# Key pages of a paged attention cache, copied ahead in DRAM and turned by float32r transposes

## The reference

```
hn   = rmsnorm(x) * (1 + sc1) + sh1          # sc, sh, gt from silu(c) @ w_ada
q, k, v, xl, gl = split(hn @ w_in)           # 8 heads of 128, LRU width 1024
attn = stick_breaking(q, k, v)               # the prompt over itself
       # sample b: its 8 tokens, then back over its 8 cached pages:
       for page in reversed(page_table[b]):  # keys and values, 128 rows x 8 heads x 128
           z = q @ cache_k[page].T * scale + bias
           w = exp(log_sigmoid(z) + sums of log_sigmoid(-z) to the right + carry)
           o += w @ cache_v[page]
lru  = rglru(conv4(xl)) * gelu(gl)
x    = x + gt1 * (concat(attn, lru) @ w_out)
x    = x + gt2 * ((gelu(ug) * uv) @ w_down)  # ug, uv = conv3(hn2 @ w_up)
```

## Time and profile before

| | |
|---|---|
| median of 3 runs | 2901.7 us |
| profiled execution, its span | 2902.6 us |
| PE busy | 2828.4 us (97%) |
| DVE, ACT, Pool busy | 1769.2, 1189.4, 280.8 us |
| key page transposes on PE, L1052 and L1056 | 2 x 256, mean 286 and 273 ns |
| page loads | 128 of 512 KB, landing after some 5 us |

### The profile page before, as it was taken

How to read it: one execution, slowest core, us unless ns; L and a number is a source line. 1 busy time by engine, 2 the same in 40 slices (tenths; PEclk the granted TensorE clock), 3 DMA queues, 4 the chain that set the end, 5 groups by cost and what they waited for, 6 DMA issues and landing times.

```text
span 2902.6 us, 60828 instructions
## 1 busy us (share of the span) xinstructions
PE 2828.4 (97%) x24051; PEld 2695.1 (93%) x24051; DVE 1769.2 (61%) x2752; ACT 1189.4 (41%) x1458; POOL 280.8 (10%) x532
## 2 busy tenths in 40 slices
PE   5999999999999999799999999999999999999999
PEld 3689999878888999699999999999999999999999
DVE  3433433544534433888888888888888755555553
ACT  3244444545444322644444444444444422222222
POOL 0000000112221000011111111111111000000000
PEclk9999999999999999899999999999999999999999
DMA  9985555377667655633333333333333633333323
GB/s 360 318 264 168 159 162 167 109 230 233 217 222 235 197 158 169 201 115 100 112 105 113 99 117 105 109 100 117 111 102 106 210 109 108 106 107 110 106 82 110
DMA packets 608980, 444.51 MB, mean 153 GB/s; under 512 B 14569, under 2 KB 556127, under 8 KB 607469
## 3 DMA queue, kind: packets, MB, share of 16 engines
q1 hardware_dynamic: 585602, 363.97, 41.2%
q0 software_dynamic: 22176, 77.86, 8.2%
q10 hardware_dynamic: 1044, 0.43, 0.1%
HBM read 408.14 MB, written 34.06 MB: 152 GB/s over the span
## 4 chain that ended last, share of the span: by engine, by line
PE 92%; DVE 3%; DMA 2%; ACT 2%; issue 1%; SPq 0%; DVEq 0%; ACTq 0%; POOLq 0%
PE ps L808 45%; PE ps L1265 36%; PE ps L824 2%; PE ps L1101 1%; PE ps L1067 1%; PE ps L1052 1%; PE ps L904 1%; PE ps L1056 1%; PE ps L932 1%; DMA wide_act<-in_w_ada_dram 1%; PE ps L848 1%; PE ps L966 1%; DMA page<-in_cache_k_dram 0%; PE ps L944 0%; DMA raw<-in_w_in_dram 0%
## 5 line engine op out<-in xcount | busy, mean ns | idle before, releaser
L1265 PE MATMUL ps<-ops,w_hi 128*128 128x288 f32 x4608 | 921.0, 296 | 0.5 <-DVE w_lo L2334 0.5
L1265 PEld LDWEIGHTS ps<-ops,w_hi 128*128 128x128 f32 x4608 | 741.7, 189 | 0.9 <-DVE w_lo L2334 0.9
L1265 PE MATMUL ps<-ops,w_lo 128*128 128x288 f32 x2304 | 679.4, 295 | 0.0
L1929 DVE TENSOR_TENSOR w_lo<-raw,w_hi 128x1024 fp32r<-128x1024 f32 x240 | 293.2, 1225 | 575.4 <-ACT w_hi L1377 575.3
L808 PE MATMUL ps<-gs,w_hi 128*128 128x288 f32 x3072 | 607.1, 294 | 0.0
L808 PE MATMUL ps<-act_hi,w_hi 128*128 128x288 f32 x1792 | 544.7, 304 | 8.4 <-DVE w_lo L1929 3.1
L808 PE MATMUL ps<-act_lo,w_hi 128*128 128x288 f32 x1792 | 528.9, 295 | 0.0
L808 PE MATMUL ps<-act_hi,w_lo 128*128 128x288 f32 x1792 | 528.1, 295 | 0.0
L1377 ACT ACTIVATE w_hi<-raw 128x1024 fp32r<-128x1024 f32 x240 | 253.4, 1058 | 657.3 <-PE ps L808 639.8
L808 PEld LDWEIGHTS ps<-gs,w_hi 128*128 128x128 f32 x3072 | 490.3, 188 | 0.0
L808 PE MATMUL ps<-gs,w_lo 128*128 128x288 f32 x1536 | 451.3, 294 | 0.0
(11 more groups left out here) (377 smaller groups left out, 3130.7 us busy)
## 6 DMA issues: line engine op xcount, KB each, us to landing
raw<-in_w_up_dram SPq DMA_DIRECT2D x120, 512.0 KB, 4.3
raw<-in_w_down_dram SPq DMA_DIRECT2D x128, 384.0 KB, 3.2
raw<-in_w_in_dram SPq DMA_DIRECT2D x80, 512.0 KB, 5.8
ada_q<-in_w_ada_dram SPq DMA_DIRECT2D x80, 512.0 KB, 5.4
page<-in_cache_v_dram POOLq DMA_DIRECT2D x64, 512.0 KB, 4.7
page<-in_cache_k_dram POOLq DMA_DIRECT2D x52, 512.0 KB, 4.7
ax<-in_w_up_dram SPq DMA_DIRECT2D x48, 512.0 KB, 4.9
wide_act<-in_w_ada_dram SPq DMA_DIRECT2D x22, 1024.0 KB, 12.2
```

The lines of the kernel that those rows point to most:

```text
L1265: mm = pe.matmul(ps[:, bank, 0:HALF], w[slot][:, kk, :], moving(i, kk, low), start=i not in ADDED and kk == 0 and w is w_hi and not low, s ...
L1929: dve.tensor_tensor(w_lo[s][:], raw[s][:], w_hi[s][:].bitcast(F32), ALU.subtract).then_inc(lo_done, 1)
```

## The change

While the q,k,v stage runs, Pool copies all 64 key pages from the cache to an internal DRAM tensor `key_save`, in the order in which they will be used, eight for each head; `COPY_AFTER` gives the number of finished blocks of its head that each of the eight waits for. The stores of a head come after its seventh copy. The key pages are later loaded from `key_save` (so at an address that needs no page number) into `keys_r`, a float32r tensor at the same place as the four homes, and turned with a float32r identity into a float32r view of the same banks. `ident_r` is made by DVE at the beginning of the LRU stage, and PE waits for it once. SP and Pool wait for all copies before they load a first key page. Value pages are loaded as before.

```diff
+COPY_AFTER = (0, 0, 1, 2, 2, 3, 4, 4)
...
 SECOND_LIFE = {
+    "sq2_used": ("filled", 2), "ident_rounded": ("consts", 2),
...
+    key_save = nc.dram_tensor("key_save", (NB * PAGES, P, NH * P), F32, kind="Internal").ap()
...
         temps.close()
+        keys_r = rounded("keys_r", [P, 4, NH, P])
         page = [tmp(f"page{i}", [P, NH, P]) for i in range(4)]
...
+        ident_r = tmp("ident_r", [P, P], F32R)
...
-            sp.wait_ge(sem("pt_loaded"), 16)
+            sp.wait_ge(sem("keys_copied"), 16 * NB * PAGES)
             for k in range(4, 16):
-                b, at = page_of(k)
-                number = sp.value_load(pt[0:1, 8 * b + at:8 * b + at + 1], min_val=0, max_val=npool - 1)
                 sp.wait_ge(sem("left_turned"), k - 3)
                 sp.wait_ge(sem("right_turned"), k - 3)
-                sp.dma_start(page[k % 4][:].rearrange("p h d -> p (h d)"),
-                             ck[bass.ds(number, 1)].rearrange("n p c -> p (n c)")) \
+                sp.dma_start(keys_r[:, k % 4].bitcast(F32).rearrange("p h d -> p (h d)"), key_save[k]) \
                   .then_inc(sem(f"early_page{k % 4}"), 16)
...
-                    mm = pe.transpose(ps[:, b0, j * P:(j + 1) * P], page[n % 4][:, j, :], ident[:])
+                    mm = pe.transpose(ps[:, b0, j * P:(j + 1) * P].bitcast(F32R), keys_r[:, n % 4, j, :], ident_r[:])
...
-                    mm = pe.transpose(ps[:, b0 + 1, j * P:(j + 1) * P], page[n % 4][:, 4 + j, :], ident[:])
+                    mm = pe.transpose(ps[:, b0 + 1, j * P:(j + 1) * P].bitcast(F32R), keys_r[:, n % 4, 4 + j, :], ident_r[:])
...
+            pe.wait_ge(sem("ident_rounded"), again("ident_rounded", 1))
             for p in range(16):
                 point(0, p)
...
             take_mod(5, M_QKV + 35, 3, 7 + NH)
+            dve.tensor_copy(ident_r[:], ident[:]).then_inc(sem("ident_rounded"), 1)
             softplus(NH)
...
+            def page_number(n):
+                b, at = page_of(n)
+                return pool.value_load(pt[0:1, 8 * b + at:8 * b + at + 1], min_val=0, max_val=npool - 1)
+
+            def copy_keys(n):
+                pool.dma_start(key_save[n], ck[bass.ds(page_number(n), 1)].rearrange("n p c -> p (n c)")).then_inc(sem("keys_copied"), 16)
...
+                if k is None:
+                    ins = pool.dma_start(page[n % 4][:].rearrange("p h d -> p (h d)"),
+                                         cvv[bass.ds(number, 1)].rearrange("n p c -> p (n c)"))
+                else:
+                    ins = pool.dma_start(keys_r[:, n % 4].bitcast(F32).rearrange("p h d -> p (h d)"), key_save[k])
+                ins.then_inc(sem(f"page_loaded{n % 4}"), 16)
...
-            with pool.Fori(1, NH) as i:
-                store(i)
             pool.wait_ge(sem("pt_loaded"), 16)
+            for i in range(NH):
+                for c in range(8):
+                    wait(pool, blk_used, 6 * i + COPY_AFTER[c])
+                    copy_keys(8 * i + c)
+                    if i and c == 6:
+                        store(i)
+            pool.wait_ge(sem("keys_copied"), 16 * NB * PAGES)
             pool.wait_ge(sem("ada_used"), 10 * NH)
             for p in range(4):
                 load(0, p)
```

More of the change, by code:

```diff
@@ L308, in tmp, with rounded @@
         return temps.enter_context(nc.sbuf_tensor(name, shape, dt))
+    def rounded(name, shape):
+        alone = ExitStack()
+        t = alone.enter_context(nc.sbuf_tensor(name, shape, F32R))
+        alone.close()
+        return t
     names = {}
@@ L1761, in _ @@
             turns(act, 4, out, 4)
-            act.wait_ge(sem("sq2_used"), 1)
+            act.wait_ge(sem("sq2_used"), again("sq2_used", 1))
             act.activation(flat2(rs2[:]), ps[:, 5:7, 0:HALF], ACT.Ln, bias=eps[:], scale=-1.0 / D).then_inc(sem("rs2_ready"), 1)
@@ L2670, in _ @@
             cvv = cache_v[0].rearrange("n p h d -> n p (h d)")
+            def page_number(n):
[3 more added lines that the diff above has]
+                pool.dma_start(key_save[n], ck[bass.ds(page_number(n), 1)].rearrange("n p c -> p (n c)")).then_inc(sem("keys_copied"), 16)
             def load(i, p):
                 k, v, n = key_page(i, p), value_page(i, p), unit(i, p)
-                b, at = page_of(v if k is None else k)
-                number = pool.value_load(pt[0:1, 8 * b + at:8 * b + at + 1], min_val=0, max_val=npool - 1)
+                if k is None:
+                    number = page_number(v)
                 if n >= 4:
@@ L2683, in load @@
                         pool.wait_ge(sem("right_turned"), uses(*q) + 1)
-                pool.dma_start(page[n % 4][:].rearrange("p h d -> p (h d)"),
-                               (cvv if k is None else ck)[bass.ds(number, 1)].rearrange("n p c -> p (n c)")) \
-                    .then_inc(sem(f"page_loaded{n % 4}"), 16)
+                if k is None:
+                    ins = pool.dma_start(page[n % 4][:].rearrange("p h d -> p (h d)"),
[3 more added lines that the diff above has]
+                ins.then_inc(sem(f"page_loaded{n % 4}"), 16)
             def gates(i):
```

## The result

The changed kernel takes 2917.05 us (median of 5 runs, 2913.61 to 2917.53); the kernel before, timed with it, 2905.45 (5 runs). The ratio is 1.0037, its 95% interval 1.0026 to 1.0049: 11 us slower, beyond the 0.2% that counts as no change. The profiled execution spans 2914.7 us, 12.1 more than before.

The account below looks back on a forecast made before the run. TensorE (PE) was taken as the bound, 92% of the chain, with DMA engines full at the q,k,v stage's beginning. 2902.6 - 10.7 + 7.4 = 2899.3, less 0.9 to the runs' median: 2898.4 us, range 2884 to 2914.

Parts of the forecast that it names:

- the price of the burst: Beginning of q,k,v stage: 13 copies in a row delay weight block 12, PE stalls 5.9 us plus 1.5 of clock: 7.4.
- The share of the weights: Beside the copies at 165.0 to 184.8 us, the hardware queue was to move 172 packets a us instead of 626.
- The packets of a copy: Copies into key_save were priced like Pool's page loads, 4 KB a row, at 84 packets a us.
- The length: Burst from 165.0 us: 13 copies, 1664 packets at 84 a us, lasting 19.8 us to 184.8.
- Chunk 8: Weight chunk queued ahead of block 12, needed at 182.9 us: claimed just in time, no stall of its own.
- The clock: After PE's idle gap before head 1's sums, lower granted clock was to cost 1.5 us.
- Rival 4: Copies cost twice a page load's packet time; burst 39.6 us, stall with clock 27.2 us, total 2918.2; chance 0.13.
- The transposes: LRU stage: 512 float32r key transposes start 85 ns apart instead of 109; 10.7 us gained with the first stretch.
- The 48 later pages: Key pages turned between LRU products, counted as PE's time: 48 x 8 x 24 ns = 9.2 us gained.
- the first stretch: First 16 key pages of the LRU stage: faster turning limited by page loads and bandwidth, 1.5 us gained.
- The copies of later heads, ident, the stores and copy 63: q,k,v stage and LRU beginning: later copies hidden, ident copy in idle DVE time, stores and last copy early enough: nothing.

Follow-up runs that it names:

- Experiment 1: Changed kernel with each key_save row 64 bytes longer, so copies go in packets of 4 KB or less: 2914.89 us, 1.0036 of the kernel before.
- experiment 2: Changed kernel with all 64 copies in heads 2 to 7, none in heads 0 and 1: 2898.13 us, 0.9978 of the kernel before.
- experiment 3: Changed kernel with copied pages turned by float32 transposes and the old identity: 2922.4 us, 1.0059 of the kernel before.
- experiment 5: Changed kernel with all copies in heads 2 to 7 and float32 transposes of the copied pages: 2905.22 us, 1.0001 of the kernel before.
- experiment 8: Changed kernel with no copies in heads 0 and 1, 15 in a row at head 3, 9 or 10 in other heads: 2908.51 us, 1.0009 of the kernel before.

## Why the prediction was wrong

- **The term that failed is the price of the burst**, in the copies' part: "13 copies are 1664 packets, at 84 a us 19.8 us", with the hardware queue at 172 rows a us beside them, and hence 7.4 us. It measured 19.1. Place and kind of wait were as forecast: the sums of head 1 waiting for DVE behind a raw block. Three sizes were off, in the same direction.
  1. *The share of the weights.* 172 rows a us came from 600 to 606 us, taken as one state. It is a mixture. From 603 to 604 us of the same trace, where the page loads hold most of the engines, the packets are

```profile
q0 software_dynamic: 90, 0.36, 86.6%
...
q1 hardware_dynamic: 96, 0.05, 16.0%
```

     about one for one, some 90 rows a us. In the other five microseconds the page loads' share is 68 to 78% and 136 to 217 rows go, so for parts of them, by inference, SP's queue alone had work. Experiment 1 shows nearly the same, 80, beside copies in 4 KB packets.
  2. *The packets of a copy.* It was taken to go like a page load, 4 KB a row. Between two contiguous pieces of DRAM it goes in 16 packets of 32 KB, so the weights had 18 rows a us, not 80. This alone was worth little (experiment 1: the sums gained 0.5 us).
  3. *The length.* 14 copies went in a row and a 15th at 185.11, where 13 were counted: blocks 8 and 9 of head 1 were finished meanwhile. And the 84 packets a us include the small ones that end each engine's share, 16 a copy, which "1664 packets" left out. 15 x 144 packets at 80 to 84 a us are 26 to 27 us, which is what both bursts lasted (to 191 or 192 us), not 19.8.

  An estimate in the prediction's own form, with the 4000 packets at 626 a us behind the burst, tells what these are worth. With the measured length alone (26.5 us at 172 rows a us) block 12 lands at 188.3 us, with the measured share alone (19.8 us at 18) at 190.6, with both at 197.1. It landed at 196.4 (issued at 166.51, 29.9 us to landing), where 185.8 was forecast. So length and share made the loss together, and neither alone.
- **A step was left out.** "Chunk 8 ... is ahead of block 12 in the queue and just in time" held only with the assumed rate. PE's longest wait, 8.8 us, is for that chunk, which it could only take at 192.78. But this cost nothing of its own, since block 12 landed later still and the sums couldn't have begun before 200.33 either way. The clock took 2.3 us behind that gap, where 1.5 was forecast.
- **Rival 4** gave 2918.2, and the kernel came out at 2917.05, but not by its mechanism: a doubled packet time. Packets of 4 KB or less went at 80 a us against 84, hardly dearer. So its closeness is luck. It had the burst 13 us too long (39.6 us against 26.5), and the share of the weights, which both the forecast and rival 4 scaled from the same row, nearly five times too high (86 against 18 rows a us).
- **The transposes** were forecast at 85 ns and took 86, with loads of 141 ns as before. Of the 10.7 us the LRU stage gave 8.6 in the profile, and 9.2 in that of experiment 2 (573.3 to 866.6); over all profiles with the new transposes it is 6.5 to 9.2. With the old transposes it gave 2.9 in experiment 3 and 0.7 in experiment 5 (572.1 to 873.9). Between the medians the transposes are worth 5.4 us (experiment 3) and 7.1 (5 and 2). The 48 later pages were counted at 8 x 24 = 192 ns each. Timeline of such a page before, and after:

```profile
640.94 0.65 PE L1052 MATMUL ps<-ident,page 128*128 128x128 f32 x4
641.43 0.60 PE L1056 MATMUL ps<-ident,page 128*128 128x128 f32 x4
641.78 0.38 PE L808 MATMUL ps<-act_hi,w_hi 128*128 128x288 f32 x1
```
```profile
750.03 0.53 PE L1061 MATMUL ps<-ident_r,keys_r 128*128 128x128 f32 x4
750.40 0.51 PE L1065 MATMUL ps<-ident_r,keys_r 128*128 128x128 f32 x4
750.74 0.37 PE L817 MATMUL ps<-act_hi,w_hi 128*128 128x288 f32 x1
```

  From the first transpose to the product behind it are 0.71 us instead of 0.84: 0.13 a page, 6.2 us for 48 instead of 9.2. The weight loads (PEld) of the same two pages tell where it went. Before, the first four take 0.39 us up to the start of the next four (640.93 to 641.32), and those 0.44 up to the product's load (641.76), 98 and 110 ns each; after, both take 0.34 (750.02, 750.36, 750.70), 85 ns each. So the 24 ns hold for the second four alone. The prediction took 109 ns from a row of L1056 and counted it for all eight; the row of L1052 in the same group lasts 0.66 us and not 0.60. Why the first four's loads stood closer already before stays open. In the first stretch, up to the 17th page, the changed kernel gained 2.9 us (602.38 to 618.61 us, 19.1 to 16.2) and experiment 2 2.1, where 1.5 was counted.
- **The copies of later heads, ident, the stores and copy 63** at nothing: right (no gap from 220 to 550 us; experiment 5).
- **The rules weighed.** The forecast had 24 ns of gain for each transpose. By the Trainium skill (TensorE: Matmul & The Clock Gate, LDWEIGHTS) a weight load of 128 columns takes 107 ns, which would have left none. The trace differs: the starts are 86 ns apart, though each load lasts 141. Of the queues the Trainium skill (DMA: Bandwidth & Descriptors, Queues, rings and completion order) says that an engine drains a whole packet, typically 9 to 17 descriptors, before it turns to the next queue. By that the weights could have had many rows in each turn. The runs show equal counts, 177 rows to 178 packets and 796 to 799, where "packet" is the profile's word for one piece. Beside the copies in 4 KB packets (9 pieces for an engine) equal counts don't tell single turns from turns of nine. Beside the 32 KB packets a copy has only two pieces for an engine, and 9 or more rows in each turn don't fit. The order on one engine is in no trace.

## What to carry to other kernels

Before adding transfers to a stage, look for the point at which several of their conditions are already met when the issuing engine gets free, and count what is then released in a row: here 15 copies of 512 KB in a row cost 19 us at a beginning with full DMA engines and 10 us in a later head, five cost nothing that shows, and 64 spread over later heads cost nothing and make the kernel faster than before (0.9978). Compare the time that a transfer takes beside a burst with how long before its use it is asked for (24 against 17 us in experiment 8). Read the share that two queues get from a stretch in which both are backed up in every slice, not from a mean over some us. And price a shortened run of instructions from its first start to the start of what follows it.

## What the hardware showed beyond that

- A copy of 512 KB between contiguous DRAM pieces went in 32 KB packets, one an engine; in 4 KB packets the same bytes took the engines about as long (15 copies in 26 to 27 us, until 191 or 192 us, in both).
- Two backed-up queues got the same number of packets: rows of 512 bytes beside pieces of 32 KB (177 to 178) and of 4 KB (796 to 799).
- SP stayed in a single DMA instruction for 18 us (experiment 8) and for 22 us (block 12 of the changed kernel) while the burst ran; that what it had issued before couldn't drain is an inference.
- The same bytes described in four pieces a row took Pool 8 to 15 us an issue instead of 1.13, and went in 4 KB and 16-byte packets instead of 32 KB ones.
- The granted clock can differ where the work is the same: behind the LRU stage 5 us of it ran at 0.50 instead of 0.74, and the profiles of three kernels of nine lost about 1.5 us there.
- The transposes' weight loads take 141 ns in float32r as in float32, against 188 for the float32r products; only the distance between starts fell.
